# Routers of a three-layer mixture kernel: VectorE splits the second token tile into high and low part, and one norm has two filler products fewer

## The chip, the cores and the metric

The kernel runs on one core of one Trainium2 chip. The metric is the device time of one launch in microseconds, as a median over several launches. The kernel is one program for the whole model; nothing is left to the host but laying out weights.

## The reference

The model takes 256 tokens of 1024 features through three layers. Each layer is a token mixer, a residual sum, a norm and a mixture of 32 experts. A router sends each token to two experts of one group. In short (`layer` 0 has an RMS norm, layers 1 and 2 a layer norm with gain and bias; layer 2 mixes by a Fourier transform, layer 1 by retention and windowed attention):

```python
h = norm(x_scaled + mixer(x) @ w_out)             # (256, 1024)
group_logits = h @ w_group                        # 4 groups
exp_logits = (h @ w_router).reshape(n_tok, 4, 8)  # 8 experts in each
# first maximum of the groups, the two largest experts in that group,
# softmax weights of both times the weight of the group
hid = silu(xs @ w_gate[e]) * (xs @ w_up[e])       # tokens xs of expert e
out[token] += weight * (hid @ w_down[e])
```

The first layer's experts have 256 hidden features, those of the other two 512. All of it is fp32.

## The kernel before, in words

Tokens lie on the 128 partitions in two tiles, j = 0 and 1. The stages follow one another, each a block of its own on all engines: an engine starts on the next block when all engines have ended the one before. The stages that matter here are:

- `stage_out_route`, three times (tags `one`, `l`, `l`): output product of the mixer, residual, norm, router logits, choice of experts, and for each chosen token its place in its expert's list. It is called a router below.
- `stage_experts` and in it `stage_packed`: for each pair of experts the tokens are gathered by a product with a one-hot matrix, go through the three weights, and are scattered back by another product.
- `stage_norm`: the layer norm behind an expert stage. With tag `b0` it stands between the second expert stage and the Fourier stage; with `b1` it is the last stage and writes the output, and has then no work on TensorE.
- `stage_fourier`: the mixer of the last layer.

In a router, TensorE multiplies tile 0's rows by `w_out` in two halves of columns, then the first half of tile 1, transposes tile 0's normed rows (`turn`), multiplies the second half of tile 1, and forms the logits of tile 0 from the transposed rows that ScalarE has moved out of PSUM (`turned_out`). Then come four filler products (`keep_busy`, 128x512 products with an identity matrix whose result nobody reads; each is two records in the trace), `turn(1)`, `logits(1)`, and six filler products. Then TensorE waits for the selection (`s_sel`, line 1549 on VectorE) and counts places with small products (line 1434, "placement products"), and two more filler products end its part. VectorE works out both norms, reads the logits (line 1534, or 1536 in the first router), finds the maxima in `first_max` (lines 1517 to 1521), forms weights and places, and in the next stage builds the one-hot matrix (line 1851), for which the gather products wait (lines 1726 and 1727).

The gather needs the normed rows as a pair of rounded parts: `k.h_high` is the row rounded to the type fp32r, `k.h_low` the rest, both laid out by feature chunk. `by_chunk(j)` is the row read in that order: the inner step is 8 elements of fp32, 32 bytes. ScalarE writes `h_high` of each tile (`high(j)`, line 1455) and signals `s_hi`; GpSimd then subtracts (line 1480) and has nothing else in this stage. `Order` (`o(...)`) makes each VectorE instruction wait for the one before.

Expert weights are streamed by SyncE's queue, in chunks of 2 MB, into a ring of 11 rooms in the second and third expert stage (8 in the first). The first 11 chunks are issued ahead, in earlier stages. Chunk 11 goes out when all products that read chunk 0 have ended (`s_used`), chunk 12 when those of chunk 1 have, and so on:

```python
if i >= room:
    sp.wait_ge(self.s_used, self.used0 + i - room + 1)
```

A chunk of the second and third expert stage is read by 8 products (16 records). In the first expert chunk these follow the gather of the first pair: 32 products with 128 columns.

Of the kernel before, what the change touches and what calls it, by code (L numbers as in the profile page):

```python
# [7 lines left out]
ALU = mybir.AluOpType  # L8
ACT = mybir.ActivationFunctionType
AX = mybir.AxisListType  # L10
F32 = mybir.dt.float32
# [5 lines left out]
NJ = T // P  # L17
# [156 lines left out]
def bc(ap, axis, n):  # L174

    shape = list(ap.shape)
    return ap.unsqueeze(axis).broadcast_to(shape[:axis] + [n] + shape[axis:])


def keep_busy(k, bank, n):  # L180

    ident = k.table("ident")
    for _ in range(n):
        k.nc.tensor.matmul(bank, ident, bc(ident, 1, W // P), start=True, stop=True)
# [1076 lines left out]
def stage_norm(k, tag, gain, bias, ahead=None, out=None):  # L1261

    nc = k.nc
    s_ld, s_inv, s_rs, s_done, s_stored = (k.sem(f"{n}_{tag}") for n in (
        "norm_rows_loaded", "inv", "rstd", "rows_done", "rows_stored"))
    scope = ExitStack()
    k.scope = scope
    with scope:
        g, b = (k.carve(k.gate_room, NJ * 3 * T + n * D, [P, D]) for n in range(2))
        stats = k.sb(f"stats_{tag}", [P, NJ, 2, 6])  # L1270
        mv, v, inv, rs = (k.sb(f"{n}_{tag}", [P, NJ, 2]) for n in ("mean_var", "var_eps", "inv", "rstd"))
        spare = k.ps(f"spare_ps_{tag}", [P, W])
        with nc.Block() as block:
            @block.tensor
            def _(pe):
                if out is None:
                    keep_busy(k, spare[:], 9)

            @block.sync
            def _(sp):  # L1280
                sp.dma_start(g, gain.broadcast_to([P, D])).then_inc(s_ld, 16)  # L1281
                sp.dma_start(b, bias.broadcast_to([P, D])).then_inc(s_ld, 16)
                if ahead is not None:
                    ahead(sp)
                if out is not None:
                    for j in range(NJ):
                        sp.wait_ge(s_done, j + 1)
                        sp.dma_start(out[0, j * P:(j + 1) * P], k.x[:, j]).then_inc(s_stored, 16)
                    sp.wait_ge(s_stored, 16 * NJ)

            @block.scalar
            def _(act):
                for j in range(NJ):
                    act.wait_ge(s_inv, j + 1)
                    nc.scalar.activation(rs[:, j, 0:1], inv[:, j, 0:1], ACT.Sqrt).then_inc(s_rs, 1)

            @block.vector
            def _(dve):
                o = Order(dve, k.order["dve"])

                def moments(j):
                    for n in range(2):
                        o(nc.vector.bn_stats(stats[:, j, n], k.x[:, j, n * W:(n + 1) * W]))
                    o(nc.vector.bn_aggr(mv[:, j], stats[:, j].rearrange("p n s -> p (n s)")))
                    o(nc.vector.tensor_scalar(v[:, j, 0:1], mv[:, j, 1:2], LN_EPS, None, ALU.add))
                    nc.vector.reciprocal(inv[:, j, 0:1], v[:, j, 0:1]).then_inc(s_inv, 1)

                def rows(j):
                    dve.wait_ge(s_rs, j + 1)
                    refine(nc, o, rs[:, j, 0:1], v[:, j, 0:1], inv[:, j, 0:1])  # L1310
                    dve.wait_ge(s_ld, 32)  # L1311
                    xj = k.x[:, j]
                    o(nc.vector.scalar_tensor_tensor(out=xj, in0=xj, scalar=mv[:, j, 0:1], in1=g,  # L1313
                                                     op0=ALU.subtract, op1=ALU.mult))
                    nc.vector.scalar_tensor_tensor(out=xj, in0=xj, scalar=rs[:, j, 0:1], in1=b,  # L1315
                                                   op0=ALU.mult, op1=ALU.add).then_inc(s_done, 1)

                moments(0)
                moments(1)
                rows(0)  # L1320
                rows(1)
                o.restart()
    k.scope = k.ctx
# [26 lines left out]
def stage_out_route(k, tag, alpha, rr, ahead):  # L1350


    nc = k.nc
# [11 lines left out]
    with scope:  # L1365
# [19 lines left out]
        def by_chunk(j):  # L1385
            return rows[:, j, :].rearrange("p (i c) -> p c i", c=KC)

        with nc.Block() as block:
            @block.sync
            def _(sp):  # L1390
                ahead(sp, s_y)
# [46 lines left out]
            @block.scalar  # L1438
            def _(act):
                def squares(j, n):  # L1440
                    if bias is None:
                        act.wait_ge(s_x, 2 * j + n + 1)
                        nc.scalar.activation(rows[:, j, n * W:(n + 1) * W], k.x[:, j, n * W:(n + 1) * W], ACT.Square,
                                             accum_out=v[:, j, n:n + 1]).then_inc(s_ss, 1)

                def turned_out(j):
                    for n in range(2):
                        act.wait_ge(s_t, 2 * j + n + 1)
                        nc.scalar.activation(k.hT[:, 4 * n:4 * n + 4, j * P:(j + 1) * P],
                                             turned[2 * j + n].rearrange("p (c t) -> p c t", c=4),  # L1450
                                             ACT.Copy).then_inc(s_ht, 1)

                def high(j):
                    act.wait_ge(s_h, j + 1)
                    nc.scalar.activation(k.h_high[:, j], by_chunk(j), ACT.Copy).then_inc(s_hi, 1)

                def root(j):
                    act.wait_ge(s_inv, j + 1)
                    nc.scalar.activation(rs[:, j, 0:1], tmp[:, j, 0:1], ACT.Sqrt).then_inc(s_rs, 1)

                squares(0, 0)
                squares(0, 1)
                root(0)
                squares(1, 0)
                turned_out(0)
                high(0)
                squares(1, 1)
                root(1)
                turned_out(1)
                high(1)  # L1470
                act.wait_ge(s_d, 1)
                nc.scalar.activation(ge[:], ge[:], ACT.Exp).then_inc(s_e, 1)
                act.wait_ge(s_d, 2)
                nc.scalar.activation(m[:, 3], m[:, 3], ACT.Exp).then_inc(s_e, 1)

            @block.gpsimd
            def _(pool):
                for j in range(NJ):
                    pool.wait_ge(s_hi, j + 1)
                    nc.gpsimd.tensor_tensor(k.h_low[:, j], by_chunk(j), k.h_high[:, j].bitcast(F32), ALU.subtract)  # L1480

            @block.vector
            def _(dve):
                o = Order(dve, k.order["dve"])
                tt, ts, stt = nc.vector.tensor_tensor, nc.vector.tensor_scalar, nc.vector.scalar_tensor_tensor
# [9 lines left out]
                def norm(j):  # L1495
                    if bias is None:
                        dve.wait_ge(s_ss, 2 * j + 2)
                        o(tt(v[:, j, 0:1], v[:, j, 0:1], v[:, j, 1:2], ALU.add))
                        o(ts(v[:, j, 0:1], v[:, j, 0:1], 1.0 / D, eps, ALU.mult, ALU.add))
                    else:  # L1500
                        o(nc.vector.bn_aggr(mv[:, j], stats[:, j].rearrange("p n s -> p (n s)")))
                        o(ts(v[:, j, 0:1], mv[:, j, 1:2], eps, None, ALU.add))
                    nc.vector.reciprocal(tmp[:, j, 0:1], v[:, j, 0:1]).then_inc(s_inv, 1)
                    dve.wait_ge(s_rs, j + 1)
                    refine(nc, o, rs[:, j, 0:1], v[:, j, 0:1], tmp[:, j, 0:1])
                    dve.wait_ge(s_gl, 16 if bias is None else 32)
                    xj = k.x[:, j, :]
                    if bias is None:
                        stt(out=rows[:, j, :], in0=xj, scalar=rs[:, j, 0:1], in1=g[:],
                            op0=ALU.mult, op1=ALU.mult).then_inc(s_h, 1)  # L1510
                    else:
                        o(stt(out=xj, in0=xj, scalar=mv[:, j, 0:1], in1=g[:], op0=ALU.subtract, op1=ALU.mult))
                        stt(out=xj, in0=xj, scalar=rs[:, j, 0:1], in1=b_row[:],
                            op0=ALU.mult, op1=ALU.add).then_inc(s_h, 1)
# [11 lines left out]
                residual(1, 0)  # L1526
                residual(1, 1)
                norm(1)
                o(nc.vector.memset(k.gates[:, :, NE:], 0.0))
                o(nc.vector.memset(k.place[:, :, NE:], -1.0))  # L1530
                dve.wait_ge(s_rl, 16 if w_bias is None else 32)
# [1184 lines left out]
```

## Time and profile before

| | us |
|---|---|
| median of 3 launches | 1940.79 |
| lowest and highest | 1939.73, 1950.39 |
| profiled execution | 1946.02 |
| its span, first to last instruction | 1944.1 |
| TensorE busy | 1803.4 (93%) |
| VectorE busy | 702.9 (36%) |
| ScalarE busy | 415.9 (21%) |
| GpSimd busy | 83.8 (4%) |
| granted TensorE clock, mean | 0.971 |

The busy times are those of the profiled execution. The granted clock is a share of full speed: 1.00 is 2.4 GHz, 0.50 is 1.2 GHz. Matmuls are pipelined, so a product's duration in a timeline is longer than its distance to the next; for a pace one takes start to start. The weights moved are 583 MB in all. The first router lies at about 469 to 519 us of the span, the second at 896 to 948, the third at 1429 to 1481; the norm `b0` at 1396 to 1412.

### The profile page before, as it was taken

How to read it: one execution, taken by the hardware profiler on the slowest of the kernel's cores; microseconds unless marked ns; L12 is line 12 of the kernel's file. 1: busy time of each engine (PE TensorE's matmuls, PEld its weight loads, DVE VectorE, ACT ScalarE, POOL GpSimd, SP SyncE). 2: the span in 40 equal slices, each digit the busy share in tenths (PEclk: the TensorE clock that was granted, in tenths of full speed). 3: DMA queues.
4: the chain of work that ended last, by engine and by line, in shares of the span. 5: the costliest groups of instructions: out<-in, count | busy, mean ns of one | idle time of the engine just before them, and what ended most of it. 6: DMA issues, size and time to landing. Idle time of an engine off the chain costs nothing. (4 is left out here: it accounts for less than half of the span.)

```text
span 1944.1 us, 20802 instructions
## 1 busy us (share of the span) xinstructions
PE 1803.4 (93%) x8550; PEld 942.8 (48%) x8550; DVE 702.9 (36%) x1389; ACT 415.9 (21%) x691; POOL 83.8 (4%) x66
## 2 busy tenths in 40 slices
PE   7999996998999998999999999988799999999885
PEld 6884444794555554555444444333255344443331
DVE  3656863345334334444322222222423122222124
ACT  2421215441322222231111111111111111111111
POOL 0000001411100000210000000000000000000000
PEclk9999998899999999999899999999898999999998
DMA  5354331008299993745599999999795999999995
GB/s 211 125 167 157 141 108 26 1 1 363 94 421 406 413 411 127 276 161 214 241 424 423 424 424 425 424 424 425 276 423 229 425 424 424 423 423 424 425 424 227
DMA packets 95522, 583.45 MB, mean 300 GB/s; under 512 B 19324, under 2 KB 21500, under 8 KB 30398
## 3 DMA queue, kind: packets, MB, share of 16 engines
q1 hardware_dynamic: 90669, 580.43, 73.0%
q10 hardware_dynamic: 4752, 1.61, 0.4%
q8 instruction: 73, 1.20, 0.3%
q14 instruction: 28, 0.22, 0.0%
HBM read 578.83 MB, written 3.15 MB: 299 GB/s over the span
## 5 line engine op out<-in xcount | busy, mean ns | idle before, releaser
L1742 PE MATMUL up_ps_l<-pool,hT 128*64 128x512 f32 x576 | 129.2, 596 | 10.8 <-DMA pool<-in_expert_w_up 10.8
L426 PE MATMUL proj_ps<-pool,hT 128*128 128x512 f32 x320 | 138.3, 592 | 0.0
L1742 PE MATMUL gate_ps_l<-pool,hT 128*64 128x512 f32 x576 | 128.9, 594 | 8.1 <-DMA pool<-in_expert_w_gate 7.9
L1763 PE MATMUL y_ps_l<-pool,hidden_l 128*64 128x512 f32 x576 | 129.2, 596 | 4.2 <-ACT hidden_l L1832 2.4
L1901 DVE SCALAR_TENSOR_TENSOR y_low_l<-y_ps_l,slot_gate_l,y_high_l 128x512 fp32r<-128x512 f32 x64 | 47.1, 751 | 195.4 <-ACT y_high_l L1842 195.4
L418 PE MATMUL proj_ps<-hT,pool 128*128 128x256 f32 x512 | 111.9, 380 | 0.0
L418 PEld LDWEIGHTS proj_ps<-hT,pool 128*128 128x128 f32 x512 | 96.9, 190 | 14.8 <-issue 1.8
L1891 DVE TENSOR_TENSOR hidden_l<-hidden_l,up_ps_l 128x512 f32<-128x512 f32 x32 | 22.0, 688 | 219.9 <-PE up_ps_l L1742 219.9
L426 PEld LDWEIGHTS proj_ps<-pool,hT 128*128 128x128 f32 x320 | 60.8, 190 | 74.4 <-issue 74.1
L1842 ACT ACTIVATE y_high_l<-y_ps_l,slot_gate_l 128x512 fp32r<-128x512 f32 x64 | 44.0, 688 | 206.4 <-PE y_ps_l L1763 202.8
L1742 PEld LDWEIGHTS gate_ps_l<-pool,hT 128*64 128x64 f32 x576 | 40.3, 137 | 93.8 <-issue 75.3
L1742 PEld LDWEIGHTS up_ps_l<-pool,hT 128*64 128x64 f32 x576 | 39.3, 137 | 91.2 <-issue 72.1
L1827 ACT ACTIVATE hidden_l<-gate_ps_l 128x512 f32<-128x512 f32 x32 | 34.9, 1090 | 214.5 <-PE turn_ps_l L1779 214.5
L1763 PEld LDWEIGHTS y_ps_l<-pool,hidden_l 128*64 128x64 f32 x576 | 39.3, 137 | 84.6 <-issue 70.9
L1866 DVE SCALAR_TENSOR_TENSOR x<-x,gather_ps_l 128x512 f32<-128x512 f32 x64 | 42.5, 685 | 99.6 <-PE gather_ps_l L1751 99.5
L1726 PE MATMUL gather_ps_l<-onehot_l,h_high_l 128*128 128x256 f32 (+1 forms) x288 | 76.6, 301 | 1.6 <-DVE onehot_l L1851 1.6
L1819 ACT ACTIVATE hT<-gather_ps_l 128x512 f32<-128x512 f32 x64 | 38.3, 598 | 182.5 <-PE gather_ps_l L1727 182.5
L1727 PE MATMUL gather_ps_l<-onehot_l,h_low_l 128*128 128x256 f32 (+1 forms) x288 | 75.3, 296 | 0.0
L1726 PEld LDWEIGHTS gather_ps_l<-onehot_l,h_high_l 128*128 128x128 f32 x288 | 59.3, 206 | 7.0 <-DVE onehot_l L1851 4.7
L1727 PEld LDWEIGHTS gather_ps_l<-onehot_l,h_low_l 128*128 128x128 f32 x288 | 59.5, 207 | 0.6
L1397 PE MATMUL out_ps_l<-store,hT 128*128 128x512 f32 x128 | 55.7, 593 | 2.4 <-PEq L2491 1.3
L1851 DVE TENSOR_TENSOR onehot_l<-tables,place 128x512 fp32r<-128x512 f32 (+1 forms) x18 | 11.4, 634 | 125.9 <-PE turn_ps_l L1779 119.8
(532 smaller groups left out, 2794.4 us busy)
## 6 DMA issues: line engine op xcount, KB each, us to landing
pool<-in_expert_w_up SPq DMA_DIRECT2D x36, 2048.0 KB, 31.9
pool<-in_expert_w_down SPq DMA_DIRECT2D x36, 2048.0 KB, 32.0
pool<-in_expert_w_gate SPq DMA_DIRECT2D x36, 2048.0 KB, 32.2
pool<-in_w_in_blocks SPq DMA_DIRECT2D x18, 2048.0 KB, 7.5
gate_room<-in_expert_w_gate SPq DMA_DIRECT2D x14, 2048.0 KB, 26.2
store<-in_expert_w_up SPq DMA_DIRECT2D x14, 2048.0 KB, 23.9
pool<-in_moe_w_gate SPq DMA_DIRECT2D x12, 2048.0 KB, 12.6
pool<-in_moe_w_up SPq DMA_DIRECT2D x12, 2048.0 KB, 12.1
```

The costliest lines, as they stand in the source:

```text
L418: last = mm(pp[:, n % 2, m * T:(m + 1) * T], wbuf[n % 2][:, c, m * P:(m + 1) * P], k.hT[:, c, :], start=(c == 0), stop=(c == KC - 1))
L426: last = mm(pp[:, n % 2, j * W:(j + 1) * W], k.hT[:, c, j * P:(j + 1) * P], wbuf[n % 2][:, c, :], start=(c == 0), stop=(c == KC - 1))
L1397: last = nc.tensor.matmul(y[:, j, n, :], k.hT[:, c, j * P:(j + 1) * P], w_out[:, c, n * W:(n + 1) * W], start=(c == 0), stop=(c == KC - 1))
L1726: mm(at, k.h_high[:, j, c], moving, start=(j == 0), stop=False)
L1727: last = mm(at, k.h_low[:, j, c], moving, start=False, stop=(j == NJ - 1))
L1742: last = mm(out[e * CAP:(e + 1) * CAP, 0:H], xg(part * r + c)[:, 0, at:at + CAP], ex.weights(i, e, c), start=(part + c == 0), stop=(part = ...
L1763: last = mm(Y[e * CAP:(e + 1) * CAP, n], hidT[:, part * r + c, e * CAP:(e + 1) * CAP], ex.weights(i, e, c)[:, n * W:(n + 1) * W], start=(p ...
L1819: nc.scalar.activation(xg(n * per[b], per[b])[:, :, 0:width], got, ACT.Copy).then_inc(s_xg, 1)
L1827: nc.scalar.activation(hid[:].rearrange("p (c n) -> p n c", c=HT), G[:, 0:H].rearrange("p (n c) -> p n c", c=HT), ACT.Silu).then_inc(s_sg, 1)
L1842: nc.scalar.activation(yh[:, n], Y[:, n], ACT.Copy, scale=slot_gate[:, 0:1]).then_inc(s_yh, 1)
L1866: nc.vector.scalar_tensor_tensor(out=xs, in0=xs, scalar=1.0 if p else alpha, in1=scatter_bank[o], op0=ALU.mult, op1=ALU.add).then_inc(s_ad ...
L1901: nc.vector.scalar_tensor_tensor(out=yl[:, n], in0=Y[:, n], scalar=slot_gate[:, 0:1], in1=yh[:, n].bitcast(F32), op0=ALU.mult, op1=ALU.sub ...
```

## The change

Two things are changed. In all three routers `high(1)` on ScalarE and the second subtraction on GpSimd are dropped; VectorE makes both parts of tile 1 itself, a copy and a subtraction, directly behind `norm(1)`. ScalarE and GpSimd go on making those of tile 0. And `stage_norm` issues seven filler products in place of nine.

```diff
@@ stage_norm
                 if out is None:
-                    keep_busy(k, spare[:], 9)
+                    keep_busy(k, spare[:], 7)
@@ stage_out_route, scalar
                 turned_out(1)
-                high(1)
                 act.wait_ge(s_d, 1)
@@ stage_out_route, gpsimd
-                for j in range(NJ):
-                    pool.wait_ge(s_hi, j + 1)
-                    nc.gpsimd.tensor_tensor(k.h_low[:, j], by_chunk(j), k.h_high[:, j].bitcast(F32), ALU.subtract)
+                pool.wait_ge(s_hi, 1)
+                nc.gpsimd.tensor_tensor(k.h_low[:, 0], by_chunk(0), k.h_high[:, 0].bitcast(F32), ALU.subtract)
@@ stage_out_route, vector
                 norm(1)
+                dve.wait_ge(s_h, 2)
+                o(nc.vector.tensor_copy(k.h_high[:, 1], by_chunk(1)))
+                o(tt(k.h_low[:, 1], by_chunk(1), k.h_high[:, 1].bitcast(F32), ALU.subtract))
                 o(nc.vector.memset(k.gates[:, :, NE:], 0.0))
                 o(nc.vector.memset(k.place[:, :, NE:], -1.0))
```

## Rows read from the trace of the kernel before

**Rows 1.** Windows, second router and behind: length, five engines busy, clock, DMA share, GB/s.
```profile
930.00:939.40 9.40, 8.48 (x37) 4.95 (x36) 5.53 (x16) 4.52 (x5) 2.85 (x1) 1.00 1.02 428
939.40:942.20 2.80, 0.01 (x1) 0.02 (x1) 2.46 (x13) 0.00 (x0) 0.00 (x0) 0.98 0.84 348
942.20:948.90 6.70, 5.92 (x15) 3.32 (x15) 2.52 (x14) 0.20 (x1) 0.00 (x0) 0.50 0.01 4
948.90:955.90 7.00, 7.00 (x33) 6.88 (x33) 0.98 (x5) 0.60 (x1) 0.00 (x0) 0.50 0.02 4
955.90:961.20 5.30, 5.30 (x19) 1.71 (x20) 0.00 (x0) 0.60 (x1) 0.00 (x0) 0.69 0.00 0
970.00:1380.00 410.00, 391.80 (x1911) 158.18 (x1907) 90.07 (x154) 63.05 (x90) 0.00 (x0) 1.00 1.01 424
```

**Rows 2.** Timeline of TensorE, second router: start, us, instruction, idle time before.
```profile
933.96 5.40 PE L184 MATMUL turned_ps_l<-tables 128*128 128x512 f32 x12
942.19 2.34 PE L1434 MATMUL place_ps_l<-sel_l,router_tables_l 128*128 128x32 f32 x10 [2.83 <-DVE sel_l L1549]
944.34 3.76 PE L184 MATMUL turned_ps_l<-tables 128*128 128x512 f32 x4
...
955.90 5.26 PE L1742 MATMUL gate_ps_l<-first_room,hT 128*64 128x512 f32 x16
```

**Rows 3.** Timeline of VectorE, second router.
```profile
934.26 0.23 DVE L1534 TENSOR_TENSOR logits_l<-logit_ps_l,router_b_l 128x72 f32<-128x72 f32 x1 [3.41 <-PE logit_ps_l L1413]
...
934.73 2.75 DVE L1518 TENSOR_TENSOR eq_l<-logits_l,max_l 128x8 f32<-128x8 f32 x1
937.52 0.17 DVE L1519 TENSOR_TENSOR eq_l<-eq_l,router_tables_l 128x8 f32<-128x8 f32 x1
...
944.67 0.23 DVE L1564 SCALAR_TENSOR_TENSOR place<-place_ps_l,sel_l 128x64 f32<-128x64 f32 x1 [0.58 <-PE place_ps_l L1434]
...
945.16 0.19 DVE L1566 TENSOR_REDUCE largest_count<-place_ps_l 128x1 f32<-128x32 f32 x1
948.40 0.42 DVE L1851 TENSOR_TENSOR onehot_l<-tables,place 128x256 fp32r<-128x256 f32 x1 [3.05 <-PEq L1388]
```

**Rows 4.** Timeline of GpSimd, second router.
```profile
934.61 2.85 POOL L1480 TENSOR_TENSOR h_low_l<-x,h_high_l 128x1024 fp32r<-128x1024 f32 x1 [11.03 <-ACT h_high_l L1455]
```

**Rows 5.** Timeline of GpSimd and VectorE, a stage ahead of the first router.
```profile
443.25 4.54 POOL L1228 TENSOR_TENSOR pool<-pool,nat 128x2048 f32<-128x2048 f32 x1 [39.80 <-ACT pool L1218]
444.76 3.05 DVE L1240 TENSOR_SCALAR comb_var<-comb_var 128x8 f32<-128x8 f32 x1
```

**Rows 6.** Timeline of TensorE, first router.
```profile
506.06 5.40 PE L184 MATMUL turned_ps_one<-tables 128*128 128x512 f32 x12
514.29 1.32 PE L1434 MATMUL place_ps_one<-sel_one,router_tables_one 128*128 128x32 f32 x10 [2.83 <-DVE sel_one L1549]
515.42 3.66 PE L184 MATMUL turned_ps_one<-tables 128*128 128x512 f32 x4
```

**Rows 7.** Timeline of VectorE, first router.
```profile
506.37 0.23 DVE L1536 COPY logits_one<-logit_ps_one 128x72 f32<-128x72 f32 x1 [3.92 <-PE logit_ps_one L1413]
```

**Rows 8.** Groups by line and form: busy us, mean ns of one, idle before.
```profile
L684 DVE TENSOR_TENSOR pool<-inverse_rows,pool 128x961 f32<-128x961 f32 x1 | 1.8, 1819 | 0.1
...
L773 DVE COPY inverse_rows<-inverse_rows 128x1024 f32<-128x1024 f32 x1 | 1.1, 1070 | 0.0
...
L1455 ACT ACTIVATE h_high_l<-x 128x1024 fp32r<-128x1024 f32 x4 | 8.2, 2060 | 0.0
```

**Rows 9.** Window behind the filler of the first router, columns as in rows 1.
```profile
519.10:528.30 9.20, 7.64 (x32) 5.49 (x32) 2.28 (x6) 4.19 (x7) 0.00 (x0) 1.00 0.00 1
```

**Rows 10.** Timeline, norm behind the second expert stage.
```profile
1400.87 10.67 PE L184 MATMUL spare_ps_b<-tables 128*128 128x512 f32 x18 [7.24 <-issue]
...
1407.52 1.28 DVE L1315 SCALAR_TENSOR_TENSOR x<-x,rstd_b,gate_room 128x1024 f32<-128x1024 f32 x1
...
1413.17 7.15 PE L2502 MATMUL dft_ps<-gate_room,x 128*128 128x256 f32 x32 [1.62 <-PEq L146]
```

## The prediction

> **What bounds the kernel now.** I read the page first: TensorE is busy 93% of the span, VectorE 36%, so averages say only that TensorE or what feeds it sets the time. The change touches four places, so I went on by stretches. Rows 1 are the windows over the second of the three router stages and what follows it. In 970 to 1380, the expert stage, the DMA share is 1.01 at 424 GB/s: the weight stream is the limit, TensorE has 18 us to spare. But from 942.2 to 961.2 the stream stands still (DMA share 0.01, 0.02, 0.00): its 11 rooms are full, and the next load waits until the first room has been read by the 16 products of the first expert chunk [rows 1, 2]. So each microsecond by which that chunk ends sooner moves the whole stream, and the end, by one. In the same stretch the granted clock is 0.98, then 0.50, 0.50, 0.69: TensorE falls to its lower level (1.2 GHz) right behind 2.8 us of idleness [rows 1].
>
> What is it idle for? The timeline of VectorE has a 128x8 product at line 1518 that takes 2.75 us, where its neighbour at line 1519, as small, takes 0.17 [rows 3]. GpSimd's subtraction for h_low runs 934.61 to 937.46; line 1518 starts at 934.73 and ends at 937.48 [rows 3, 4]. The earlier combine stage shows the same: a 128x8 operation of 3.05 us on VectorE ends at 447.81, a GpSimd product at 447.79 [rows 5]. I read both as VectorE waiting for GpSimd. Selection (line 1549) follows and releases TensorE at 942.19, 2.83 us after its filler products ended at 939.36 [rows 2].
>
> **The change, part by part.**
>
> *The second subtraction leaves GpSimd.* Line 1518 falls from 2.75 to 0.17: 2.58 us sooner for selection, once in each of the three routers; TensorE idles the same 2.83 us in the first [rows 3, 6]. The filler ends at 939.36 and the placement products would start at 942.19 - 2.58 = 939.61, so TensorE waits 0.25 us in place of 2.83. In the first router the filler ends at 511.46 and they would start at 514.29 - 2.58 = 511.71 [rows 6].
>
> *High and low part go to VectorE, behind the norm.* Its cover there is the idleness before line 1534, 3.41 us (second and third router), or line 1536, 3.92 us (first) [rows 3, 7]; logits depend on TensorE and ScalarE alone. The two new operations read x in steps of 32 bytes, which no VectorE row shows. Nearest above in kind: the fp32 copy of 1024 elements with steps of 128 bytes takes 1.07 us, and the product that reads 961 elements with such steps takes 1.82, so 1.94 us for 1024 [rows 8]. Pair: 3.01, with two gaps of 0.03 and the wait, 3.1 us. Upper bound: the same two jobs on the engines that do them now, 2.06 on ScalarE and 2.85 on GpSimd, 4.9 us [rows 4, 8]. Any lower price hides too. I take 3.1, as these rows are VectorE's own with steps: hidden, with 0.3 us to spare in two routers and 0.8 in the first. Without cover each would cost 3.1 us.
>
> What it reads is steps of eight fp32 words, and the Trainium skill (Vector Engine (DVE) Microarchitecture Reference, section 5.2, "Measured stream behaviour on trn2") has a port at full rate only in runs of two adjacent words; it gives 2.5 ns per column at steps of 24 words and about 1.75 at 72 or more. By 2.5 the subtraction would take some 2.7 us and the pair 4.2, an estimate from that page: 0.8 us late in two routers, and the sum 1.6 to 2 us smaller. The rows with steps, 1.89 ns per element, agree in direction; none has these steps.
>
> *ScalarE* loses 2.06 us behind the last eviction; its next work, a table load and an exponential, wait for VectorE's selection, so nothing is gained there. GpSimd was waited for only at line 1518. The two memsets move behind the pair, within its cover. No DMA and no queue moves.
>
> *The clock.* Today the fall comes behind 2.83 us of idleness. TensorE keeps 1.00 through 930 to 939.4, which has 0.9 us of idleness and 24 small products between filler; and behind 1.58 us of idleness in the first router [rows 1, 9]. After the change the longest gaps would be 0.25 us before the placement products, then, as today, 0.8 us before the gather (948.10 to 948.88; 1.6 in the first router). I therefore take the clock as held. What it is worth:
> - Placement products: 2.15 us start to start at 0.50, 1.13 in the first router at about full clock [rows 2, 6]: 1.0 us in each later router.
> - Last filler (four records): 3.66 and 3.76 us at the lower level; four at 0.45, from 12 in 5.40, are 1.84: 1.8 to 1.9 us, all three [rows 2, 6].
> - Gather of the second and third: 32 products in 7.0 us at 0.50 [rows 1]. At 1.00 between half of that (3.5) and 32 times the 0.113 us of a small product at 1.13 for ten (3.6), with a start of 0.1: I take 3.7, so 3.3 us. The first gather runs at 1.00 already.
> - First expert chunk of those two: 5.26 us now [rows 2]. The granted clock over these 5.3 us is 0.69, so they hold 3.66 us of full clock [rows 1]: 1.6 us.
>
> VectorE's own end has to be early enough. In the second router line 1566 ends at 945.35 [rows 3]; less 2.58, less the 0.58 wait for placement, 942.2. TensorE's filler would end at 939.6 + 1.1 + 1.84 = 942.6, so TensorE stays last at the block's end, and the one-hot starts 0.30 us behind it as today (948.10 to 948.40) [rows 2, 3].
>
> *Two products fewer in the norm.* This filler serves only the norm after the second expert stage, where TensorE runs until 1411.54 and VectorE ends at 1408.80; the Fourier stage starts at 1413.17 [rows 10]. Two products are four records at 0.45: 1.8 us off the path, and TensorE (1409.7) is still the last. The last norm has no filler. The stream has its ring full before 1473 whatever happens here, so this moves the restart too.
>
> **Sum.** First router 2.58 + 1.82 = 4.4. Second and third, each 2.58 + 1.0 + 1.9 + 3.3 + 1.6 = 10.4. Norm 1.8. Together 4.4 + 20.8 + 1.8 = 27.0 us. The stream must be idle at its new restart: 950.8 in the second router, and its fill ends by about 942 [rows 1]: it is, with 8 us left. Both expert stages behind it are bound by it from the first chunk on, and the first expert stage follows TensorE, so nothing takes this back. Against the profiled execution (1946.02, its span 1944.1 and 1.9 around it): 1919.0. The median of the runs shown is 1940.79, 5.2 below that execution; I carry the difference over whole: 1913.8, so 1914.
>
> **The rivals.**
>
> *The clock falls all the same.* For: the placement products are tiny, and two short gaps lie around 1.84 us of filler. Against: the stretches that kept it [rows 1, 9]. Left are 3 x 2.58 + 1.8 = 9.5 us: 1931.
>
> *The clock holds for placement and filler but not through the 128-column gather and the gap before it.* For: this gather ran 7 us at 0.50 without bringing the clock back [rows 1]. Left: 4.4 + 2 x (2.58 + 1.0 + 1.9) + 1.8 = 17.2 us: 1924.
>
> *The pair outlasts its cover.* At 4.9 us it ends 1.5 us late in two routers and 1.0 in the first. With the clock held, 27 - 4 = 23: 1918; TensorE then idles 1.75 us before placement, near what it has borne, so it may also lose the clock: 9.5 - 4 = 5.5: 1935. Against: both rows of VectorE with steps are faster.
>
> *Slower than before.* The same mechanism with no floor: the pair costs its excess over the cover in each router. With the clock lost it eats the 9.5 us at 6.7 us a pair (2 x 3.3 + 2.8 = 9.4). At 10 us a pair the excesses are 19.3, 9.8 more than comes in: 1951. For: the steps are unseen on this engine. Against: that is twice what the slowest engine needs.
>
> *Line 1518 does not wait for GpSimd.* Then only the norm's 1.8 us come, 1939. Against: here and in the combine stage both end together to 0.02 us [rows 3 to 5].
>
> **How the numbers follow.** Clock held throughout 0.55 (1914); held until the gather 0.18 (1924); fallen 0.12 (1931); pair late 0.10 (1918 to 1935); slower 0.03; no wait there 0.02. The predicted time is the first. Its own range is 1910 to 1919: 0.3 us an item and the late pair of the page's figure. The range that leaves out less than 2 in 10 is 1910 to 1931. What a measurement of this kernel tells from no change is about 0.5%, 9.7 us: faster is below 1931.1. The fallen clock lies on that line and is shared: faster 0.55 + 0.18 + 0.06 + 0.05 = 0.84; same 0.06 + 0.05 + 0.02 = 0.13; slower 0.03.
>
> **What the profile after will show.** Line 1518 at 0.17 us in all three routers. Copy and subtraction on VectorE near 1.1 and 1.9 us, and line 1534 still idle before it, for TensorE. The placement products within 0.3 us of the filler's end. Granted clock 1.00 from there through the gather, which takes about 3.7 us. The stream still for some 8 us in place of 19. In the norm TensorE ends 1.8 us sooner. Wrong would make it: a clock of 0.50 behind the placement products, a line 1534 that no longer waits, or a stream that is idle or short later in the expert stages.

## The result, and the profile after

The changed kernel takes 1927.91 us (median of 4 launches, 1926.73 to 1929.74), the kernel before 1940.26 in the same comparison (4 launches, 1936.95 to 1950.39): a ratio of 0.9939 [0.991, 0.9969], 12 us faster. The profiled execution took 1929.74 (span 1927.6, mean granted clock 0.978; before 0.971). The prediction was 1914, 27 us less than 1940.79. Faster was right, and 1928 lies in the range of 1910 to 1931, but less than half of the forecast gain came: the clock was not held as forecast.

Timeline of VectorE in the changed kernel, second router, and below the "..." the third router's logits (start, us, instruction, idle time before). These answer to [rows 3]:

```profile
931.98 1.14 DVE L1528 CAST h_high_l<-x 128x1024 fp32r<-128x1024 f32 x1
933.15 2.02 DVE L1529 TENSOR_TENSOR h_low_l<-x,h_high_l 128x1024 fp32r<-128x1024 f32 x1
...
935.51 0.23 DVE L1535 TENSOR_TENSOR logits_l<-logit_ps_l,router_b_l 128x72 f32<-128x72 f32 x1
...
935.97 0.17 DVE L1516 TENSOR_TENSOR eq_l<-logits_l,max_l 128x8 f32<-128x8 f32 x1
...
1456.42 0.23 DVE L1535 TENSOR_TENSOR logits_l<-logit_ps_l,router_b_l 128x72 f32<-128x72 f32 x1 [0.37 <-PE logit_ps_l L1413]
```

The pair takes 3.19 us from start to end (931.98 to 935.17), and the 128x8 product that took 2.75 us (now line 1516) takes 0.17. The cover is used up: of the 3.41 us of idleness before the logits [rows 3] nothing is left in the second router and 0.37 us in the third, where TensorE ran slower.

Timeline of TensorE, second router, against [rows 2]:

```profile
935.21 5.40 PE L184 MATMUL turned_ps_l<-tables 128*128 128x512 f32 x12
940.84 1.30 PE L1434 MATMUL place_ps_l<-sel_l,router_tables_l 128*128 128x32 f32 x10 [0.24 <-DVE sel_l L1550]
941.98 1.96 PE L184 MATMUL turned_ps_l<-tables 128*128 128x512 f32 x4
944.72 0.33 PE L1727 MATMUL gather_ps_l<-onehot_l,h_high_l 128*128 128x128 f32 x1 [0.78 <-DVE onehot_l L1852]
```

The idleness before the placement products is 0.24 us in place of 2.83; they, the last filler and the 32 products of the gather run at the upper level. Windows of the same stretch and of the third router's end (columns as in [rows 1]):

```profile
942.00:945.00 3.00, 2.22 (x9) 0.92 (x8) 2.01 (x9) 0.00 (x0) 0.00 (x0) 1.00 0.40 167
945.00:949.00 4.00, 4.00 (x36) 3.64 (x37) 0.75 (x4) 1.05 (x2) 0.00 (x0) 1.00 0.03 6
949.00:954.00 5.00, 5.00 (x26) 1.65 (x24) 0.00 (x0) 0.14 (x1) 0.00 (x0) 1.00 0.19 36
...
1454.00:1458.00 4.00, 3.97 (x19) 2.94 (x20) 3.26 (x12) 1.86 (x3) 0.00 (x0) 0.70 1.01 428
1458.00:1462.00 4.00, 4.00 (x10) 1.81 (x9) 3.37 (x17) 0.28 (x2) 0.00 (x0) 0.88 1.01 420
1462.00:1466.00 4.00, 3.75 (x17) 1.96 (x15) 1.95 (x10) 0.01 (x1) 0.00 (x0) 1.00 0.66 274
1466.00:1471.00 5.00, 4.47 (x32) 4.48 (x32) 1.48 (x6) 0.60 (x1) 0.00 (x0) 0.82 0.00 0
1471.00:1477.00 6.00, 6.00 (x17) 1.76 (x18) 0.00 (x0) 0.60 (x1) 0.00 (x0) 0.58 0.00 0
```

The second router is what the prediction described: granted clock 1.00, and a stream that stands still for about 10 us (40% of 942 to 945 and 19% of 949 to 954 are busy) in place of 19. The third is not: the clock is 0.70 in the stretch of the transposes and logits, comes back, and falls again inside the gather, so that the first expert chunk ran at 0.58. It took 6.08 us there, as TensorE's timeline shows beside the filler and the late products of the gather:

```profile
1456.09 6.82 PE L184 MATMUL turned_ps_l<-tables 128*128 128x512 f32 x12
1462.75 1.20 PE L1434 MATMUL place_ps_l<-sel_l,router_tables_l 128*128 128x32 f32 x10
...
1469.03 0.28 PE L1727 MATMUL gather_ps_l<-onehot_l,h_high_l 128*128 128x128 f32 x1
1469.28 0.42 PE L1727 MATMUL gather_ps_l<-onehot_l,h_high_l 128*128 128x128 f32 x1
...
1471.12 6.08 PE L1743 MATMUL gate_ps_l<-first_room,hT 128*64 128x512 f32 x16
```

The norm behind the second expert stage, against [rows 10]:

```profile
1391.87 9.07 PE L184 MATMUL spare_ps_b<-tables 128*128 128x512 f32 x14 [7.40 <-issue]
1402.57 7.14 PE L2503 MATMUL dft_ps<-gate_room,x 128*128 128x256 f32 x32 [1.62 <-PEq L146]
```

From the filler's start to the Fourier stage it is 10.70 us now and was 12.30.

One measure serves for all that follows: in each router, from the first transpose of the second token tile (line 1405) to the end of the first expert chunk, where the stream restarts. In the two profiled executions this is 29.1, 30.4 and 30.4 us before, and 24.8, 20.1 and 24.6 after: 4.3, 10.3 and 5.8 gained, 20.4 in all, and 1.6 in the norm. The spans differ by less, 16.5 us (1944.1 and 1927.6), mostly because this stretch of the first router begins 4.9 us later in the changed kernel's execution (507.83 against 502.97), in code that is the same (another 0.6 us lies between this stretch and the next router's). The clock falls there too. The delay is there early, 5.2 us at a VectorE instruction of line 632, and the granted clock of 19 to 145 us was 1.00 before and 0.97 after. Window and instruction, before and then after:

```profile
19.00:145.00 126.00, 124.07 (x577) 105.17 (x576) 67.73 (x131) 37.20 (x42) 0.00 (x0) 1.00 0.40 143
142.46 1.14 DVE L632 TENSOR_SCALAR pool<-store,conv_w 128x256 f32<-128x256 f32 x4
```

```profile
19.00:145.00 126.00, 124.08 (x563) 104.79 (x562) 62.84 (x120) 36.04 (x41) 0.00 (x0) 0.97 0.40 143
147.67 1.14 DVE L632 TENSOR_SCALAR pool<-store,conv_w 128x256 f32<-128x256 f32 x4
```

### The profile page after: what moved, and what is told of

It reads as the page before. It is cut to its first block and busy times, and to the rows that moved or that the text cites. A ratio compares the mean times of both kernels' runs of the same rounds, so it can differ in the third digit from the quotient of the medians.

```text
span 1927.6 us, 20794 instructions
## 1 busy us (share of the span) xinstructions
PE 1794.6 (93%) x8546; PEld 937.3 (49%) x8546; DVE 704.5 (37%) x1395; ACT 409.5 (21%) x688; POOL 75.4 (4%) x63
## 5 line engine op out<-in xcount | busy, mean ns | idle before, releaser
L1743 PE MATMUL up_ps_l<-pool,hT 128*64 128x512 f32 x576 | 129.2, 596 | 10.7 <-DMA pool<-in_expert_w_up 10.7
L426 PEld LDWEIGHTS proj_ps<-pool,hT 128*128 128x128 f32 x320 | 60.8, 190 | 74.4 <-issue 74.1
L1727 PE MATMUL gather_ps_l<-onehot_l,h_high_l 128*128 128x256 f32 (+1 forms) x288 | 71.3, 287 | 1.6 <-DVE onehot_l L1852 1.6
L1728 PE MATMUL gather_ps_l<-onehot_l,h_low_l 128*128 128x256 f32 (+1 forms) x288 | 70.0, 283 | 0.0
L1727 PEld LDWEIGHTS gather_ps_l<-onehot_l,h_high_l 128*128 128x128 f32 x288 | 55.4, 192 | 5.4 <-DVE onehot_l L1852 3.2
L1728 PEld LDWEIGHTS gather_ps_l<-onehot_l,h_low_l 128*128 128x128 f32 x288 | 55.6, 193 | 0.6
L1743 PE MATMUL up_ps_l<-store,hT 128*64 128x512 f32 x224 | 50.6, 597 | 5.2 <-DMA store<-in_expert_w_up 5.2
## 6 DMA issues: line engine op xcount, KB each, us to landing
pool<-in_moe_w_gate SPq DMA_DIRECT2D x12, 2048.0 KB, 12.5
```

Of the source, the lines that this page charges most:

```text
L426: last = mm(pp[:, n % 2, j * W:(j + 1) * W], k.hT[:, c, j * P:(j + 1) * P], wbuf[n % 2][:, c, :], start=(c == 0), stop=(c == KC - 1))
L1727: mm(at, k.h_high[:, j, c], moving, start=(j == 0), stop=False)
L1728: last = mm(at, k.h_low[:, j, c], moving, start=False, stop=(j == NJ - 1))
L1743: last = mm(out[e * CAP:(e + 1) * CAP, 0:H], xg(part * r + c)[:, 0, at:at + CAP], ex.weights(i, e, c), start=(part + c == 0), stop=(part = ...
```

## The experiments

**What does one launch say? The change and its parts again.** Four kernels in one comparison, each also profiled: the kernel before and the kernel after once more, and each of the two independent edits alone: the norm's edit, below, in the kernel before, and all of the change but this edit.

```diff
-                    keep_busy(k, spare[:], 9)
+                    keep_busy(k, spare[:], 7)
```

> The unchanged kernel once more, for a second profile of it. Theory A (chance of the clock): the profiled launch of before was a dear one, 1946.0 against a median of 1940.3; in this profile at least one of the three routers keeps its clock at 1.00 behind the 2.8 us of idleness or gets it back sooner, and the stretch from the transposes of tile 1 to the end of the first expert chunk is shorter than the 30.4 us of the second and third router there. Theory B (the clock falls each time, and the change loses elsewhere what it gains): all three routers fall as before, 30.4 us in the second and third within 1 us, and the difference between launches lies ahead of the first router.

> The changed kernel once more. Theory A: ratio 0.990 to 0.996, as in its first timing; the stretch from the transposes of tile 1 to the end of the first expert chunk is 20 us where the clock holds (second router of the first profile) and up to 24.5 where it falls in the gather (third), and which router falls is another one in this profile. Theory B: the same router falls again, the third, and the first and second hold.

> Only the split on VectorE, nine filler products in the norm. If the norm's 1.8 us is real in the median: 1.8 us over the changed kernel, ratio to before about 0.9948 with 0.9939 for the changed kernel. Rival: the norm's cut gives nothing in the median, since a shorter filler leaves a colder clock to the Fourier stage: same as the changed kernel.

> Only the norm's two filler products fewer. Both theories: 1.8 us faster, ratio 0.9991, too small to tell in the times; in the profile the filler is four records shorter and its end leads the Fourier stage's start by the same 1.6 us. Rival: a granted clock under 1.00 in the Fourier stage, and no gain.

| kernel | median (lowest to highest), launches | ratio to before [95%] | stretch in the three routers of its profile, us |
|---|---|---|---|
| before, again | 1942.74 (1934.16 to 1947.4), 10 | 1.0001 [0.9981, 1.0021] | 29.1, 25.5, 22.7 |
| after, again | 1928.41 (1923.67 to 1929.87), 6 | 0.9925 [0.9903, 0.9947] | 24.8, 23.4, 24.6 |
| split alone | 1927.69 (1925.85 to 1928.8), 6 | 0.9922 [0.9901, 0.9943] | 24.8, 20.1, 23.4 |
| norm alone | 1938.33 (1934.31 to 1947.58), 12 | 0.9989 [0.997, 1.0009] | 29.1, 30.4, 23.0 |

The gain belongs to the split. The norm's edit can't be told from nothing in the times. In these profiles the norm takes 10.7 us with 7 products and 11.6 to 12.5 with 9, about 1.4 us. The profiles of all the runs below show less. In four of the eight profiles with 7 products (after with 3, subtraction twice, gap filled again, both filled) the filler ended before VectorE did, TensorE idled 1.9 to 2.6 us in place of 1.6 to 1.7, and the first products of the Fourier stage ran at a clock of 0.80 to 0.82; in the other four, and in all five with 9, they ran at 1.00. The rows of after, again and of after with 3:

```profile
1401.33 7.14 PE L2503 MATMUL dft_ps<-gate_room,x 128*128 128x256 f32 x32 [1.62 <-PEq L146]
1402.49 8.72 PE L2503 MATMUL dft_ps<-gate_room,x 128*128 128x256 f32 x32 [2.51 <-PEq L146]
```

From the end of the second router's stretch to the start of the third's, a part in which the norm is the only difference (but for one filler product in both filled), it is 501.1 us on average over the five profiles with 9 (500.0 to 502.1) and 500.4 over the eight with 7 (500.0 to 500.7). So 0.7 us is the better estimate of what the norm's edit brings. The rival put down for it, a colder clock in the Fourier stage, came true in half of the profiles.

The surprise is the unchanged kernel. Its later routers took 30.4 us both times in the execution from which I predicted, and 25.5 and 22.7 here. Windows of the unchanged kernel's new execution, second router and then third, placement with last filler and the gather:

```profile
953.10:959.80 6.70, 5.92 (x15) 3.32 (x15) 2.52 (x14) 0.20 (x1) 0.00 (x0) 0.52 0.01 5
959.80:963.50 3.70, 3.70 (x33) 3.63 (x33) 0.98 (x5) 0.60 (x1) 0.00 (x0) 1.00 0.01 2
1479.20:1483.10 3.90, 3.11 (x15) 1.81 (x15) 2.54 (x14) 0.20 (x1) 0.00 (x0) 1.00 0.01 4
1483.10:1486.80 3.70, 3.70 (x32) 3.63 (x32) 0.98 (x5) 0.60 (x1) 0.00 (x0) 1.00 0.00 0
```

```profile
1479.21 1.30 PE L1434 MATMUL place_ps_l<-sel_l,router_tables_l 128*128 128x32 f32 x10 [2.84 <-DVE sel_l L1549]
```

In the second router the clock came back before the gather; in the third it never fell, behind the same 2.84 us of idleness. So the fall is not what the stall always costs, and part of the price that I set on it was a price of that one execution. The third router of norm alone shows a third course: the clock fell among the transposes and logits (0.71), the filler took so long that no idleness was left before the placement products, and they and the gather ran at 1.00. The changed kernel varies too: in its first profile the clock fell in the third router's gather, in the second profile in both later ones.

The routers are not the only place where launches differ. In the thirteen profiles of this document the first router's stretch begins between 502.97 and 513.78 us of the span, though no edit touches what runs before it. The profile from which I predicted has the earliest start of all.

**The clock without the stall, and the stall without the clock.** In the kernel before, three filler products more ahead of the wait for the selection fill the stall's 2.83 us; in the kernel after, three fewer open a gap as long as the stall was (the same line with 3 for 6).

```diff
                 logits(1)
-                keep_busy(k, tp[:, 0], 6)
+                keep_busy(k, tp[:, 0], 9)
                 pe.wait_ge(s_sel, 1)
```

> The kernel before with nine filler products ahead of the selection wait in place of six: TensorE works until some 0.1 us before selection, and VectorE's 2.75 us at line 1518 stays. It separates the clock from the stall. Theory A (before loses the clock behind the idleness in most launches, and dearly): the clock holds behind the filler in all three routers; placement to gather takes 4.7 us in the first and 3.9 in the others in place of 6.4 and 6.7, and the kernel gains 5 to 10 us, ratio 0.995 to 0.997. Theory B (the clock is worth little in a typical launch): within 2 us of before.

> The changed kernel with three filler products ahead of the selection wait in place of six, so that TensorE idles 2.9 us there as it did before the change, while line 1518 stays short. Theory A: the clock falls again behind the idleness; placement to gather takes 6.4 and 6.7 us again, and the kernel keeps only the stall and the norm, some 9.5 us: 1932 where the changed kernel has 1928. Theory B: no different from the changed kernel, 1928.

Before with 9: 1934.02 (1926.74 to 1937.93, 12 launches), ratio 0.9965 [0.9946, 0.9985], 6.8 us. After with 3: 1933.36 (1927.01 to 1942.21, 12 launches), ratio 0.9962 [0.994, 0.9985], 5.0 to 5.5 us above the two medians of the kernel after. The timelines of before with 9, second router, show VectorE's stall still there, and TensorE's wait covered:

```profile
939.25 2.75 DVE L1518 TENSOR_TENSOR eq_l<-logits_l,max_l 128x8 f32<-128x8 f32 x1
...
938.49 7.97 PE L184 MATMUL turned_ps_l<-tables 128*128 128x512 f32 x18
946.71 1.30 PE L1434 MATMUL place_ps_l<-sel_l,router_tables_l 128*128 128x32 f32 x10 [0.25 <-DVE sel_l L1549]
```

Windows of after with 3, the stretches behind the gap in the first and the second router:

```profile
514.50:521.70 7.20, 5.62 (x15) 3.02 (x15) 3.31 (x13) 0.20 (x1) 0.00 (x0) 0.52 0.00 1
521.70:530.90 9.20, 9.20 (x32) 6.70 (x32) 0.96 (x5) 4.18 (x7) 0.00 (x0) 0.82 0.00 0
942.50:946.40 3.90, 3.10 (x15) 1.80 (x15) 2.53 (x14) 0.20 (x1) 0.00 (x0) 1.00 0.65 269
946.40:950.10 3.70, 3.70 (x32) 3.65 (x32) 0.99 (x5) 0.60 (x1) 0.00 (x0) 1.00 0.01 2
```

The same gap, 2.82 and 2.81 us, cost 4.1 us of clock in the first router (7.20 + 9.25 us where the kernel after has 4.68 + 7.72) and none in the second. The stretches are 27.4, 22.7 and 26.0 us in before with 9 and 28.9, 20.1 and 20.5 in after with 3. Neither run is the pure case, since the clock fell in one later router of the first, and behind the gap held in both of the second (in the third router it fell to 0.82 among the transposes and logits, so that the gap there was 1.57 us). Nor do these two profiles stand for their medians: that of before with 9 took 1937.06, among the dearest of its launches, and that of after with 3 took 1927.01, the cheapest of its own. The times size what the clock brings at 5 to 7 us in all three routers together, with a wide margin (2.9 to 10.5 by the interval of before with 9); the prediction had 17.5. After with 3 keeps the split and the norm and gains 7.4 us (0.0038 of 1940.85) where the prediction put 9.5 on the stall and the norm. And a filler edit alone brings the kernel before about half of the change's gain.

**Does VectorE wait for GpSimd, and where?** The work is left as it was in the kernel before; GpSimd's second subtraction is only held back until the selection is made.

```diff
                     pool.wait_ge(s_hi, j + 1)
+                    if j:
+                        pool.wait_ge(s_sel, 1)
```

> The kernel before, but GpSimd makes its second subtraction only when selection is done; ScalarE still makes the high part. If line 1518 waits for GpSimd's use of the memory: line 1518 takes 0.17 us, and another VectorE operation with two inputs behind selection takes up to 2.8 us in its place; placement starts 2.6 us sooner, and of the changed kernel's gain all but the norm's 1.8 us and what the later stall costs comes back (ratio 0.993 to 0.996). If line 1518 is long for a reason of its own (the first read of what TensorE wrote): it stays at 2.75.

Measured 1941.85 (1937.64 to 1950.12, 12 launches), ratio 1.0004 [0.9984, 1.0024]: of the gain that was expected (0.993 to 0.996) nothing came. Timelines of VectorE and GpSimd, second router:

```profile
945.40 0.17 DVE L1520 TENSOR_TENSOR eq_l<-logits_l,max_l 128x8 f32<-128x8 f32 x1
...
950.62 2.61 DVE L1556 TENSOR_SCALAR max_l<-max_l 128x2 f32<-128x2 f32 x1 [0.27 <-ACT max_l L1474]
```

```profile
950.36 2.85 POOL L1482 TENSOR_TENSOR h_low_l<-x,h_high_l 128x1024 fp32r<-128x1024 f32 x1 [16.11 <-DVE sel_l L1551]
```

The old place takes 0.17 us, and an operation on 128x2 that takes 0.17 in the kernel after now takes 2.61 and ends at 953.23, GpSimd's at 953.21. The same happens in the other two routers (2.60 and 2.61 us). The stall follows GpSimd's subtraction. It is not free in its new place, though: VectorE now finished its block last, TensorE waited 2.87 us before the gather (5.97 us after the placement products, not 3.88), and the clock fell there (0.51 in the gather of the second router, 0.71 in the third). The stretches are 28.4, 27.1 and 25.5 us.

**How much cover was left?** The kernel after with the subtraction issued twice.

```diff
                 o(tt(k.h_low[:, 1], by_chunk(1), k.h_high[:, 1].bitcast(F32), ALU.subtract))
+                o(tt(k.h_low[:, 1], by_chunk(1), k.h_high[:, 1].bitcast(F32), ALU.subtract))
```

> The changed kernel with VectorE's subtraction made twice, 2.0 us more behind the norm, where the pair left 0 to 0.4 us of cover in the later routers and 0.6 in the first. If the pair is hidden just so: selection comes 1.4 us later in the first router and 1.6 to 2.0 later in the others, TensorE idles 1.6 to 2.3 us ahead of placement, and the kernel is 5 us slower than the changed one, 1933, or 8 if the clock goes too. Rival: there is hidden room elsewhere, and it costs under 2 us.

Measured 1940.2 (1935.45 to 1945.68, 12 launches), ratio 0.9998 [0.9979, 1.0018]: 2 us of VectorE in each router undo the whole change. That is 12 us above the kernel after, where 5 to 8 were expected. Timelines of VectorE and TensorE, second router:

```profile
939.21 2.01 DVE L1530 TENSOR_TENSOR h_low_l<-x,h_high_l 128x1024 fp32r<-128x1024 f32 x1
...
941.51 0.23 DVE L1536 TENSOR_TENSOR logits_l<-logit_ps_l,router_b_l 128x72 f32<-128x72 f32 x1
```

```profile
946.84 1.79 PE L1434 MATMUL place_ps_l<-sel_l,router_tables_l 128*128 128x32 f32 x10 [2.23 <-DVE sel_l L1551]
```

The idleness is back, 1.74 us in the first router and 2.23 and 2.24 in the others, and with it the clock's fall in two of three (28.7, 29.9 and 22.1 us). The idleness alone is 5.5 us more than in the kernel after; the rest goes with the clock.

**Can the clock be held?** The changed kernel idles 0.78 us before the gather. First two filler products there (one in the first router), then, with it, a fifth filler product ahead of the second tile's transposes in the later routers (the second edit below).

```diff
+                keep_busy(k, TP[:], 2 if len(ex.batches[0]) > 1 else 1)
                 gather(0, 0, groups[0])
...
-                keep_busy(k, tp[:, 0], 4)
+                keep_busy(k, tp[:, 0], 4 if bias is None else 5)
                 turn(1)
```

> The changed kernel with filler in the gap between the router's end and the gather: one product (two in the first expert stage) at the head of the expert stage, where TensorE waits 0.8 us (1.6) for the one-hot matrix. Nothing else waits for it unless it outlasts the gap by up to 0.1 us. If the gap ahead of the gather's 128-column products costs the clock there: the gather to the first chunk takes 3.7 us and the chunk 3.7 in both later routers, and the kernel is 2 to 4 us faster than the changed one, 1925. If the gather's own products lose it: no difference.

> The changed kernel with one or two filler products at the head of the expert stage, once more, for a second profile and a narrower time. If the filler in that gap holds the clock through the gather: the gather again takes 4.0 us and the first chunk 3.7 in both later routers, and the median is 1 to 3 us under the changed kernel's 1928. If the first profile was chance: 5 us and 5.7 us in one of the two, and 1928.

> The changed kernel with filler in both gaps of the later routers: five products in place of four ahead of the transposes of tile 1 (TensorE waits 0.64 us there for the norm), and the one or two products at the head of the expert stage. If the two gaps are what costs the changed kernel its clock in the later routers: 20.5 us from the transposes to the end of the first expert chunk in both, at a granted clock of 1.00, against 20.1 to 24.6 in the changed kernel, and a median 2 to 4 us under it, 1924 to 1926. Rival: the small products themselves lose it, and some router still takes 23 to 25 us.

| kernel | median (lowest to highest), launches | ratio to before [95%] | stretches, us |
|---|---|---|---|
| gap filled | 1926.95 (1924.49 to 1934.01), 8 | 0.9946 [0.9919, 0.9972] | 25.2, 20.4, 21.6 |
| gap filled, again | 1926.71 (1925.99 to 1929.14), 6 | 0.9932 [0.9907, 0.9956] | 25.2, 20.4, 23.3 |
| both filled | 1925.22 (1920.53 to 1932.19), 6 | 0.9925 [0.9897, 0.9953] | 25.2, 20.4, 20.4 |

With the gap filled the gather ran at 1.00 in all four later routers, and what was left of the loss was the fall among the transposes and logits (0.83 and 0.71 in the third router). Whether the filler did it is open: with it the gather lost its clock in none of six later routers (both filled included), and without it in 5 of the 13, over all runs, that came to the gap at 1.00. If the filler did nothing, six of six would still come about one time in nine. With both filled, windows over each router from its transposes to behind the gather or the start of the first chunk:

```profile
505.42:525.00 19.58, 18.81 (x80) 11.64 (x79) 11.56 (x45) 5.77 (x10) 0.00 (x0) 1.00 0.35 146
929.62:946.37 16.75, 15.96 (x86) 10.72 (x85) 11.34 (x45) 3.38 (x6) 0.00 (x0) 1.00 0.67 280
1450.03:1466.77 16.74, 15.96 (x86) 10.72 (x85) 11.32 (x45) 3.38 (x6) 0.00 (x0) 1.00 0.67 280
```

This is the only profile with no fall in any router, and the lowest median of all, but 2.7 us below the kernel after is less than these comparisons separate: the intervals overlap almost whole, and the ratio, 0.9925, is the one that the unfilled kernel had when it was repeated. The gain of 2 to 4 us expected of the filler isn't shown by any of the three.

## Why the prediction was wrong, and where it was right

**The wait for GpSimd: right.** The 2.58 us came off at the named line in all three routers, and the stall moved with the subtraction when that was moved.

**The pair on VectorE: right.** Copy 1.14 and subtraction 2.02 us, 3.19 with gaps, against 3.1 forecast (1.07, 1.94). It is hidden, in the second, third and first router, with 0, 0.37 and 0.60 us to spare; where the third router ran at full clock (split alone) it had 0 as well. The kernel's own row at steps of 128 bytes, 1.89 ns per element, was near [rows 8]: here it is 1.97 at steps of 32 bytes, 8 words. The Trainium skill (Vector Engine (DVE) Microarchitecture Reference, section 5.2) gives 2.5 ns per column where both sources, or the destination alone, step by 24 words; here one source steps by 8 words, for which it has no figure, so the 4.2 us worked out from it in the prediction was an estimate for another pattern, and the trace decides. (That estimate also makes the copy longer in the same ratio, which it doesn't say.)

**The first router: right.** 4.3 us against 4.4; its length before (29.1) is the same in all three profiles with the routers as before.

**The order at the block's end: right.** TensorE stays last, the one-hot follows its filler, and the end of the first chunk moves the stream one for one: the second router's start to the third's changed by 11.9 us in the two profiled executions (1463.24 less 930.75 against 1452.63 less 932.00), which is that router's 10.3 and the norm's 1.6.

**The norm: smaller than said.** 1.8 us forecast, 1.6 in the first pair of profiles, 0.7 on average over all thirteen, not to be seen in the times. "TensorE (1409.7) is still the last" failed in four of eight profiles, where VectorE ended last and the Fourier stage began at the lower clock in part.

**The clock: wrong in size.** The step that failed is "I therefore take the clock as held", with the prices of 10.4 us for each later router that hang on it. Over the two later routers of the three profiles with the routers as before (before, before again, norm alone), the stretch is 27.1 us on average (30.4, 30.4, 25.5, 22.7, 30.4, 23.0), not 30.4; over those of the three with the split (after, after again, split alone) it is 22.7 (20.1, 24.6, 23.4, 24.6, 20.1, 23.4), not 20.1. That is 4.4 us for each, in place of 10.4. The prices themselves were right for the case that they describe: from a router with the clock lost all through to one with it held it is 30.4 - 20.1 = 10.3 us. What was wrong is that each launch was taken to be that case. The miss has two halves:

- 3.3 us for each: before did not always lose its clock, or not for so long. I had one execution and read its two equal routers as the rule.
- 2.6 us for each: after does not always hold it. It falls inside the gather of 128 columns in four of the six later routers, and among the transposes and logits in two of these four. This is the rival "the clock holds for placement and filler but not through the 128-column gather", in part. Of the numbers, its 1924 and the 1931 of the rival in which the clock falls all the same lie on either side of the result, 4 and 3 us away.

By these sizes the sum is 4.3 + 2 x 4.4 + 0.7 = 13.8 us, where the times give 11.9 (0.9939) and 14.5 (0.9925). The averages rest on three profiles each.

**The difference of 5.2 us "carried over whole": wrong, and it hid the first half.** The profiled execution was dear because its clock had fallen (mean granted clock 0.971, where launches near the median have 0.973 to 0.977). The same falls were in my 10.4 us: its two later routers took 60.8 us together, where the three profiles of unchanged routers average 54.1, and that is more than the whole difference, since the code ahead of its first router took 4.3 us less than their average. I counted them as gain and subtracted them once more with the median; without this second count the forecast would have been 1919.

What stays open: why the clock falls in one launch and holds in the next behind the same instructions. The runs show that it does, not what decides it.

## What to carry to other kernels

A granted clock that falls in a stretch of small products is one draw: before pricing it, look at the stretch in several executions, or compare the profiled execution's time with the spread of the launches, and don't carry that difference over when the gain you forecast is made of the same falls. Two engines whose operations end within 0.02 us of each other, the one tiny and the other long, are one wait; take the long one off, but count the cover of what replaces it to the tenth of a microsecond, for past it each microsecond comes back with the clock's on top. Filler in a gap of 2.8 us is worth trying by itself: here it brought about half of the change's gain without the change. In gaps of 0.8 us no gain could be told, and taking filler out is not free either: two products fewer in the norm saved less than their own time.

## What the runs showed of the hardware

- VectorE's stall behind GpSimd's subtraction (2.85 us) ends with it, however small VectorE's operation is: one on 128x2 is held for 2.61 us, one on 128x8 for 2.75 [rows 3].
- The unchanged kernel's launches lie between 1934.10 and 1949.08 us in one comparison (23 launches), the lowest at a mean granted clock of 0.978 and the highest at 0.970: launches of one kernel differ by 15 us. The clock goes with them, though not strictly (0.979 at 1936.42).
- Behind 2.8 us of idleness ahead of the placement products TensorE's clock fell to its lower level in eight of ten routers and stayed at 1.00 in two, with the same instructions (the third router of before again, the second of after with 3). Behind 0.78 us it held at first, and in four of the six later routers of the three profiles with the split it fell in the middle of the gather, which has no gap.
- From steps of 32 bytes VectorE's copy of 1024 elements to fp32r takes 1.12 to 1.14 us, little more than half of the 2.06 that ScalarE takes for the same [rows 8].
